# The MLP's up projection with its weights stationary and the tokens moving

## The reference

```python
h = h + merged @ w_out[l]                                  # (256, 2048)
hn = rms_norm(h, norm_mlp_w[l])                            # h * rsqrt(mean(h*h)) * w
h = h + jnp.square(jax.nn.relu(hn @ w_up[l])) @ w_down[l]  # w_up (2048, 8192), w_down (8192, 2048)
return rms_norm(h, norm_final_w)
```

## Time and profile before

| | |
|---|---|
| median of three runs | 2155.92 us (2152.78 to 2156.43) |
| span of the profiled execution | 2154.7 us |
| PE busy, share of the span | 2110.9 us, 98% |
| PEld busy | 1747.7 us, 81% |
| DVE busy | 1316.6 us, 61% |
| ACT busy | 981.6 us, 46% |
| DMA, mean | 174 GB/s |
| the MLP loop in the trace | from about 1430 us to about 2144 us |

### The profile page before, as it was taken

The page is one execution under the profiler, slowest core; times in us unless marked ns, Lnnn a source line. Parts: engine busy times, 40 slices in busy tenths (PEclk is TensorE's granted clock), DMA queues, the critical chain, the costliest instruction groups (busy, mean ns, idle before and its releaser), DMA issues.

```text
span 2154.7 us, 29089 instructions
## 1 busy us (share of the span) xinstructions
PE 2110.9 (98%) x9886; PEld 1747.7 (81%) x9886; DVE 1316.6 (61%) x1669; ACT 981.6 (46%) x1355; POOL 191.6 (9%) x224
## 2 busy tenths in 40 slices
PE   7999999999999999999999999999999999999997
PEld 6888888888888887778878878888888888888886
DVE  5646666666664577776677766555555545555554
ACT  5434545444443455554355544444434434443443
POOL 3000000000000023331033310000000000000000
PEclk9999999999999999999999999999999999999999
DMA  7656454545456655556655556556666566556664
GB/s 233 190 161 176 140 172 136 175 136 175 136 170 192 181 150 147 149 151 196 185 146 147 155 188 196 193 182 187 188 191 186 190 191 190 185 190 187 188 191 136
DMA packets 195431, 374.87 MB, mean 174 GB/s; under 512 B 16048, under 2 KB 16144, under 8 KB 194960
## 3 DMA queue, kind: packets, MB, share of 16 engines
q1 hardware_dynamic: 193152, 365.87, 56.3%
q0 software_dynamic: 2160, 7.79, 1.1%
q10 hardware_dynamic: 32, 0.01, 0.0%
HBM read 371.52 MB, written 2.10 MB: 173 GB/s over the span
## 4 chain that ended last, share of the span: by engine, by line
PE 51%; issue 41%; POOL 2%; DVE 2%; ACT 1%; DMA 1%; DVEq 1%; ACTq 0%; SPq 0%; POOLq 0%
PE acc L279 15%; PE acc L281 14%; PE acc L280 14%; PE x L809 1%; DMA raw<-w_in 1%; PE tr L302 1%; POOL MH L595 1%; POOL ML L595 1%; PE x L736 1%; PE x L691 1%; PE tr L759 1%; DVE lo L246 1%; POOL XTOK L602 0%; PE tr L764 0%; PE x L799 0%
## 5 line engine op out<-in xcount | busy, mean ns | idle before, releaser
L246 DVE TENSOR_TENSOR lo<-raw,hi 128x1024 fp32r<-128x1024 f32 (+1 forms) x696 | 866.3, 1253 | 624.7 <-ACT hi L239 613.0
L239 ACT ACTIVATE hi<-raw 128x1024 fp32r<-128x1024 f32 (+1 forms) x696 | 726.6, 1051 | 680.1 <-PE acc L281 656.9
L279 PE MATMUL acc<-hi,LAh 128*128 128x512 f32 x1856 | 735.2, 396 | 5.0 <-DVE lo L246 5.0
L281 PE MATMUL acc<-hi,LAl 128*128 128x512 f32 x1856 | 724.4, 390 | 0.0
L280 PE MATMUL acc<-lo,LAh 128*128 128x512 f32 x1856 | 723.4, 390 | 0.0
L279 PEld LDWEIGHTS acc<-hi,LAh 128*128 128x128 f32 x1856 | 349.1, 188 | 83.3 <-issue 6.9
L281 PEld LDWEIGHTS acc<-hi,LAl 128*128 128x128 f32 x1856 | 348.6, 188 | 73.8
L280 PEld LDWEIGHTS acc<-lo,LAh 128*128 128x128 f32 x1856 | 349.2, 188 | 71.3 <-issue 1.7
L279 PE MATMUL acc<-hi,LBh 128*128 128x512 f32 x896 | 352.1, 393 | 4.2 <-DVE LBl L334 2.9
L280 PE MATMUL acc<-lo,LBh 128*128 128x512 f32 x896 | 349.4, 390 | 0.0
L281 PE MATMUL acc<-hi,LBl 128*128 128x512 f32 x896 | 349.3, 390 | 0.0
(11 more groups left out here) (271 smaller groups left out, 1267.2 us busy)
## 6 DMA issues: line engine op xcount, KB each, us to landing
raw<-w_in SPq DMA_DIRECT2D x304, 512.0 KB, 3.7
raw<-w_up SPq DMA_DIRECT2D x128, 512.0 KB, 4.1
raw<-w_down SPq DMA_DIRECT2D x128, 512.0 KB, 4.2
raw<-w_proj_ssm SPq DMA_DIRECT2D x64, 512.0 KB, 4.1
raw<-w_proj_nsa SPq DMA_DIRECT2D x32, 512.0 KB, 3.7
raw<-w_out SPq DMA_DIRECT2D x32, 512.0 KB, 4.3
GA<-x SPq DMA_DIRECT2D x4, 512.0 KB, 5.7
GA<-cmp_k_w POOLq DMA_DIRECT2D x4, 512.0 KB, 8.8
```

The source lines that it names most:

```text
L239: act.activation(hi[:, sl, :, 0:n], raw[:, sl, :, 0:n], ACT.Copy).then_inc(s_hi, 1)
L246: dve.tensor_tensor(lo[:, sl, :, 0:n], raw[:, sl, :, 0:n], hi[:, sl, :, 0:n].bitcast(F32), ALU.subtract).then_inc(s_lo, 1)
L279: pe.matmul(o, xh, wh, start=(k == 0), stop=False)
L281: x = pe.matmul(o, xl, wh, start=False, stop=(k == KT - 1))
```

## The change

The up projection is done the other way round. `mm_chunk_t` takes 128 by 128 blocks of the weights as stationary operand and the 256 tokens of `LBh`, `LBl` as moving operand. The result is channel-major: each 512-wide chunk gives four blocks of 128 hidden channels by 256 tokens, two side by side in each PSUM bank. A group now has 24 products of 256 columns instead of 12 of 512.

The square needs no turn any more. But the norm factor is now one for each column, so it can't be an engine's factor for each partition. POOL stores the 256 factors to HBM (`rs_row`) and reads them back spread over all partitions (`RSB`, a part of the buffer `W`), and DVE multiplies both banks by that row. One DVE instruction then does ReLU and square, ACT copies the square to `LAh` (now from SBUF, 1024 elements at once), DVE subtracts for `LAl`. ACT doesn't take a bank in the up chunks any more.

```diff
+        def mm_chunk_t(pe, C, par, Lh, Ll, need=None):
+            pe.wait_ge(s_acc, C - 1)
+            for j in range(8):
+                for (se, v) in (need or {}).get(j, ()):
+                    pe.wait_ge(se, v)
+                pe.wait_ge(s_lo, 8 * C + j + 1)
+                sl = j % RING
+                for kk in range(2):
+                    k = 2 * j + kk
+                    for n in range(4):
+                        o = acc[par][n // 2][:, (n % 2) * S:(n % 2 + 1) * S]
+                        wh, wl = hi[:, sl, kk, n * P:(n + 1) * P], lo[:, sl, kk, n * P:(n + 1) * P]
+                        pe.matmul(o, wh, Lh[:, k, :], start=(k == 0 and n % 2 == 0), stop=False, skip_group_check=True)
+                        pe.matmul(o, wh, Ll[:, k, :], start=False, stop=False, skip_group_check=True)
+                        x = pe.matmul(o, wl, Lh[:, k, :], start=False, stop=(k == KT - 1), skip_group_check=True)
+                x.then_inc(s_mm, 1)
...
+        RSB = W[:, 0, 0:S]
...
 # POOL
-            for n, o in ((1, RS[:, 2:4]), (2, RS[:, 0:2])):
-                pool.wait_ge(s_v, n)
-                pool.tensor_tensor(o, VV[:, 0:2], mhalf[:, 0:2], ALU.pow).then_inc(s_pow, 1)
+            pool.wait_ge(s_v, 1)
+            pool.tensor_tensor(RS[:, 2:4], VV[:, 0:2], mhalf[:, 0:2], ALU.pow).then_inc(s_pow, 1)
+            pool.wait_ge(s_pow, 10)
+            pool.dma_start(rs_row.rearrange("(t p) -> p t", p=P), RS[:, 2:4],
+                           allow_slow_non_contiguous=True).then_inc(s_rso, 16)
+            pool.wait_ge(s_rso, 16)
+            pool.dma_start(RSB, rs_row.partition_broadcast(P)).then_inc(s_rsb, 16)
+            pool.wait_ge(s_v, 2)
+            pool.tensor_tensor(RS[:, 0:2], VV[:, 0:2], mhalf[:, 0:2], ALU.pow).then_inc(s_pow, 1)
...
 # PE
                 for k in range(4):
-                    hooks = {2: [lambda: pe_turn(pe, e + k - 1, Y, [(s_ff, 4 * i + k)])]} if k else {}
-                    mm_chunk(pe, C + k, (C_MLP + k) % 2, LBh, LBl, hooks, need={6: [(s_trd, E_MLP)]})
+                    mm_chunk_t(pe, C + k, (C_MLP + k) % 2, LBh, LBl, need={6: [(s_trd, E_MLP)]})
                 for k in range(4):
-                    hooks = {} if k else {2: [lambda: pe_turn(pe, e + 3, Y, [(s_ff, 4 * i + 4)])]}
-                    mm_chunk(pe, C + 4 + k, (C_MLP + k) % 2, LAh, LAl, hooks, need={6: [(s_trd, e + 4)]})
+                    mm_chunk(pe, C + 4 + k, (C_MLP + k) % 2, LAh, LAl, {},
+                             need={} if k else {2 * b: [(s_ffl, 4 * i + b + 1)] for b in range(4)})
...
 # ACT
-            act.wait_ge(s_pow, 10)
+            def high_parts(i, k):
+                act.wait_ge(s_ff, 4 * i + k + 1)
+                act.activation(LAh[:, 4 * k:4 * k + 4, :].rearrange("p a s -> p (a s)"),
+                               Y[:, :, :].rearrange("p t n -> p (t n)"), ACT.Copy).then_inc(s_ffh, 1)
...
-                    hk[8 * k + 7] = [lambda k=k: take(C + k, (C_MLP + k) % 2, XR[:, 0, :], func=ACT.Relu, scale=RS[:, 2:3])]
-                    hk[8 * k + 10] = [lambda k=k: act_split_t(act, e + k, LAh, 4 * k)]
+                    hk[8 * k + 8] = [lambda k=k: high_parts(i, k)]
...
 # DVE
-            dve.wait_ge(s_pow, 10)
-            def mlp_rows(C, par, xa):
-                dve.wait_ge(s_xa, xa)
-                dve.tensor_scalar(XR[:, 1, :], acc[par][1][:, :], RS[:, 3:4], 0.0, ALU.mult, ALU.max).then_inc(s_acc, 1)
-                dve.drain()
-                dve.tensor_tensor(Y[:, :, :], XR[:, :, :], XR[:, :, :], ALU.mult).then_inc(s_ff, 1)
+            dve.wait_ge(s_rsb, 16)
+            def squares(C, par):
+                dve.wait_ge(s_mm, 8 * C + 8)
+                for b in range(2):
+                    x = dve.tensor_tensor(XR[:, b, :].rearrange("p (c s) -> p c s", c=2),
+                                          acc[par][b][:, :].rearrange("p (c s) -> p c s", c=2),
+                                          RSB.unsqueeze(1).broadcast_to([P, 2, S]), ALU.mult)
+                x.then_inc(s_acc, 1)
+                dve.drain()
+                dve.scalar_tensor_tensor(Y[:, :, :], XR[:, :, :], 0.0, XR[:, :, :], ALU.max, ALU.mult).then_inc(s_ff, 1)
+            def low_parts(i, k):
+                dve.wait_ge(s_ffh, 4 * i + k + 1)
+                dve.tensor_tensor(LAl[:, 4 * k:4 * k + 4, :].rearrange("p a s -> p (a s)"),
+                                  Y[:, :, :].rearrange("p t n -> p (t n)"),
+                                  LAh[:, 4 * k:4 * k + 4, :].rearrange("p a s -> p (a s)").bitcast(F32),
+                                  ALU.subtract).then_inc(s_ffl, 1)
...
-                    hk[8 * k + 7] = [lambda k=k: mlp_rows(C + k, (C_MLP + k) % 2, XA_UP + 4 * i + k + 1)]
-                    hk[8 * k + 10] = [lambda k=k: dve_split_t(dve, e + k, LAh, LAl, 4 * k)]
+                    hk[8 * k + 7] = [lambda k=k: squares(C + k, (C_MLP + k) % 2)]
+                    hk[8 * k + 9] = [lambda k=k: low_parts(i, k)]
```

## The result

The changed kernel takes 2172.74 us (median of four runs, 2172.36 to 2173.55); the kernel before, timed beside it, 2156.01 us. The ratio is 1.0082, with a 95% interval of 1.007 to 1.0095: it is slower by 16.7 us, where 7.5 us of gain were forecast. The time lies outside the range of 2143.5 to 2160.

A forecast was written before the change was run, and what follows sets the result against it. The prediction took PE's instruction list to bound the MLP loop. Its terms, -14.3 + 0.5 + 4.8 + 1.5 = -7.5 us, on 2155.9 gave 2148.4 us, with an 8-in-10 range of 2143.5 to 2160.

The forecast's parts named there:

- What bounds: In the MLP loop PE's instruction list ends the stage; PE stands still for only 1.25 us out of 700.
- The turns: In the MLP loop, dropping 16 turns of eight transposes, 0.89 us each, takes 14.3 us off PE's list.
- The halves: In up chunks, 1536 products of 512 columns become 3072 of 256, loads hidden: +0.5 us, at most +5.
- The sequencer: In the up chunks, PE's sequencer takes under 10 ns an instruction, so it isn't the bound.
- Rival 3: In the up chunks, PE's instruction sequencer bounds each load and product at 0.124 us: +33 us, 2182 us; chance 0.04.
- DVE and ACT: Behind an up chunk, their evacuation and splitting work costs nothing; PE's slack of 4 us or more covers it.
- The spread: Before the MLP loop, DVE waits for the norm factors' HBM trip, 3.6 + 4.0 us; PE stands 4.8 us.
- The clock: Behind PE's stand at the fourth group, a stretch at half clock adds 1.5 us, bounds 0 and 3.0.
- Rival 2: In the up chunks, the weight load becomes the bound, 9 ns more a pair: +28 us, 2176 us; chance 0.12.
- rival 1: Before the loop, slow DMAs (5.2 us each), half clock and visible loads eat the gain: about 2155 us; chance 0.18.

The follow-up runs named there:

- the late wait: The changed kernel, but DVE waits for the spread norm factors at their first use behind the first up chunk, not before the loop: 2161.03 us, ratio 1.0026.

## Why the prediction was wrong, step by step

**What bounds: right.** PE's list ends the stage in every run, and each difference is found again in PE's starts.

**The turns: right.** -14.3 us forecast, -14.7 measured. The rest of the 15.8 us that the run without turns won are pauses that it doesn't have.

**The halves: the step that failed.** I took +0.5 us and an upper bound of +5; it is +20.4. The step was "one each 0.113 us, half of 0.227", from one burst of seven products in the first chunk, and from it that a load of 112 "fills 0.098 of 0.113 and nothing shows". The same chunk has other bursts. The one two microseconds later, in the trace of the kernel before, and under it the burst of the earlier trace rows itself in the trace of the changed kernel, where the first chunk is the same:

```profile
17.47 0.28 PE L659 MATMUL acc<-LAl,hi 128*112 128x256 f32 x1
...
17.94 0.28 PE L660 MATMUL acc<-LAh,lo 128*112 128x256 f32 x1
```

```profile
15.21 0.28 PE L690 MATMUL acc<-LAh,lo 128*112 128x256 f32 x1
...
15.92 0.28 PE L690 MATMUL acc<-LAh,lo 128*112 128x256 f32 x1
```

Four steps take 0.47 us and six take 0.71, 0.118 each. The first of these was there to be read. I took the faster burst for the rule. The bound was at fault as well: I put the price of a load and a product that both run without a pause at the larger of the two, 0.112 and 0.113, with 3 ns of hand-over. Measured is 0.120, more than either. What the runs show in its place, for 256 moving columns: beside a full load of 128 a step of 0.120, once a round is under way, in every round of the five runs that have this form; beside a narrower load either 0.1133 or 0.1178, and a round keeps the one it begins with (32 columns: three rounds and one; 112 columns: one round and seven, in two runs). For 224 columns beside 128 it is 0.112, the pace of full loads behind one another. So the full width of the load is what brings 0.120 here. Inside PE the cause stays open: the place of the moving buffer and the PSUM region are excluded as a reason, what picks between the two paces isn't known, and no run halved the products with the activations still stationary.

**The sequencer: right.** Rival 3 would hold every pair at one price, 0.124 us. With 224 moving columns full pairs start 0.112 apart, under that and under the 0.120 of the changed kernel. The sequencer isn't the bound. The page "TensorE: Matmul & The Clock Gate" of the Trainium skill, section "Wait — 56ns, not 53.3ns?", gives about 62 ns for a matmul alone; the 0.124 was my estimate, which charged the load the same. The trace contradicts the estimate, and no run here tests the 62 ns. (Rival 3's total should read 2181, not 2182.)

**DVE and ACT: right.** No wait of PE for either behind the fourth group of the first up chunk.

**The spread: right in its mechanism, too small.** The stand came where it was forecast, at the fourth group of the first up chunk, released by DVE's split behind the DMA. I took 3.6 + 4.0 us for the two DMAs and 4.8 for the stand, with an upper bound of 7.6; measured are 8.2 and 4.8 from issue to use, and 9.8. The spread was well priced by a row of the same kind. The store was priced by loads, also the 1 KB of positions with as many pieces of 4 bytes, 4.2 us, and a store of such pieces costs about twice that.

**The clock: right in its mechanism, the size in part by luck.** 1.5 us forecast, 1.6 measured. The forecast took one row as it was. In the run with the store in pairs the stretch at half clock behind the stand was longer, though the stand was shorter:

```profile
1441.01:1446.90 5.89, 5.89 (x28) 5.89 (x28) 3.35 (x3) 0.36 (x1) 0.00 (x0) 0.51 0.78 250
```

27 products begin in it, so it cost 5.89 - 27 x 0.120 = 2.6 us.

The measured terms, -14.7 + 20.4 + 9.8 + 1.6, sum to +17.1 us. The loop's first and last product in the changed kernel:

```profile
1428.96 0.37 PE L302 MATMUL acc<-LBh,hi 128*128 128x256 f32 x1
...
2159.13 0.39 PE L286 MATMUL acc<-hi,LAl 128*128 128x512 f32 x1
```

From the one to the other it takes 730.2 us, 17.5 more than the kernel before; 0.4 are left without a name. The spans differ by only 16.5 because this execution came to the loop 1.0 us earlier, in work that the change doesn't touch. Rival 2 was the case that came true, with 6.7 ns a pair where I had put 9, and rival 1's slow round trip came on top. I gave them 0.12 and 0.18, as if they excluded each other.

## What to carry to other kernels

Where the stationary side is the one that changes with each product, the moving side should be long: at 512 columns a full load was no slower than a narrow one, at 256 the full load's pace was 6% over half of the 512-column step. Before such a pace is read from a trace, read all its bursts, and every round of a loop, not one. A value that has to go through HBM to change its layout should go in few pieces, and the wait for it belongs at its first use, behind work that is ready.

## What the runs showed of the hardware

- A full load and a product of 256 columns take 0.120 us together, though full loads follow one another each 0.112 beside short products and products of 256 columns each 0.113 beside narrower loads.
- With 256 moving columns and 32 or 112 columns of load the same instructions ran at 0.1133 in some rounds and at 0.1178 in others, and no round changed its pace under way.
- A load of 32 columns beside 512 moving ones was slower than one of 128, by 5 ns a product.
- A store to HBM of 256 pieces of 4 bytes took 7.9 us from issue to landing in the changed kernel, 9.5 with the late wait and 9.8 from ACT's queue, one of 128 pieces of 8 bytes 3.5. Reading the row back over 128 partitions took 4.6 in the changed kernel and 3.2 to 4.7 in these others.
- After a stand of 9.65 us PE ran 3.5 us at half clock, after one of 2.95 us 3.3 us, and after one of 4.66 us 5.9 us: the length of the stand did not set that of the slow stretch.
